# The compressed branch's output made turned and gated on the probabilities, and added by VectorE as it reads the attention's accumulator

## The reference, cut to what matters

```
s = einsum('bgrtd,bgcd->bgrtc', qh, kcmp) * scale
s = where(cmask, s - slopes * dcmp, NEG)
p_cmp = softmax(s, axis=-1) * cmask
o_cmp = einsum('bgrtc,bgcd->bgrtd', p_cmp, vcmp)
imp = einsum('bgrtc,cj->bgtj', p_cmp, overlap)      # picks the blocks of the selected branch
...
gt = sigmoid(gates.reshape(B, S, 3, G, R).transpose(2, 0, 3, 4, 1))[..., None]
o = gt[0] * o_cmp + gt[1] * o_sel + gt[2] * o_win
```

## Time and profile before

| | |
|---|---|
| Median of 3 runs | 3756.53 us (3756.47 to 3762.29) |
| The profiled execution | 3753.49 us |
| Its span, first to last instruction | 3751.6 us |
| Mean granted PE clock | 0.955 of full speed |
| PE busy | 3490.3 us (93%) |
| DVE busy | 1752.8 us (47%) |
| ACT busy | 871.6 us (23%) |
| POOL busy | 1041.0 us (28%) |

### The profile page before, as it was taken

The page is one execution under the profiler, slowest core; times in us unless marked ns, Lnnn a source line. Parts: engine busy times, 40 slices in busy tenths (PEclk is TensorE's granted clock), DMA queues, the critical chain, the costliest instruction groups (busy, mean ns, idle before and its releaser), DMA issues. The chain is left out here.

```text
span 3751.6 us, 55639 instructions
## 1 busy us (share of the span) xinstructions
PE 3490.3 (93%) x23230; PEld 2892.4 (77%) x23230; DVE 1752.8 (47%) x2597; ACT 871.6 (23%) x1261; POOL 1041.0 (28%) x498
## 2 busy tenths in 40 slices
PE   5999999989999889999999799978996899999997
PEld 4878888867888778888888677757784778888886
DVE  4762566424887535655555535234433322323223
ACT  2111222122444112111111220244431211111112
POOL 4332333343110442212122143221212422121221
PEclk7999999999999989999999899979997899999998
DMA  3453334342000422322222164310002111111111
GB/s 95 141 177 126 113 110 125 108 121 86 12 5 1 143 65 93 112 67 73 84 78 78 45 174 106 115 58 20 20 3 107 45 50 57 39 56 45 45 45 45
DMA packets 310492, 289.74 MB, mean 77 GB/s; under 512 B 21492, under 2 KB 277030, under 8 KB 309086
## 3 DMA queue, kind: packets, MB, share of 16 engines
q1 hardware_dynamic: 282992, 202.89, 18.4%
q10 hardware_dynamic: 26482, 82.06, 5.8%
q0 software_dynamic: 816, 1.88, 0.3%
HBM read 223.22 MB, written 63.57 MB: 76 GB/s over the span
## 5 line engine op out<-in xcount | busy, mean ns | idle before, releaser
L719 POOL TENSOR_TENSOR ffn_wlo<-ffn_raw,ffn_whi 128x1024 fp32r<-128x1024 f32 x88 | 211.2, 2402 | 1061.8 <-ACT ffn_whi L913 1006.1
L209 PE MATMUL up<-h_hi,ffn_whi 128*128 128x512 f32 x1408 | 438.4, 393 | 17.1 <-POOL h_lo L410 11.2
L209 PE MATMUL up<-h_lo,ffn_whi 128*128 128x512 f32 x1408 | 435.9, 391 | 0.0
L209 PE MATMUL up<-h_hi,ffn_wlo 128*128 128x512 f32 x1408 | 435.5, 391 | 0.0
L209 PE MATMUL acc<-h_hi,whi 128*128 128x512 f32 x1136 | 371.3, 408 | 46.7 <-POOL wlo L171 24.1
L209 PE MATMUL acc<-h_lo,whi 128*128 128x512 f32 x1136 | 355.3, 394 | 0.0
L209 PE MATMUL acc<-h_hi,wlo 128*128 128x512 f32 x1136 | 353.7, 393 | 0.0
L192 POOL TENSOR_TENSOR whi<-raw,ones 128x1024 fp32r<-128x1024 f32 (+1 forms) x83 | 156.9, 1890 | 698.5 <-PE acc L209 538.0
L209 PEld LDWEIGHTS up<-h_hi,ffn_whi 128*128 128x128 f32 x1408 | 264.1, 189 | 72.5 <-issue 11.7
L209 PEld LDWEIGHTS up<-h_hi,ffn_wlo 128*128 128x128 f32 x1408 | 265.7, 189 | 55.9
L209 PEld LDWEIGHTS up<-h_lo,ffn_whi 128*128 128x128 f32 x1408 | 265.5, 189 | 56.0
(11 more groups left out here) (551 smaller groups left out, 6105.6 us busy)
## 6 DMA issues: line engine op xcount, KB each, us to landing
raw<-w_in SPq DMA_DIRECT2D x51, 512.0 KB
projT<-proj_stage ACTq DMA_DIRECT2D x51, 512.0 KB, 3.1
ffn_ada_raw<-w_ada SPq DMA_DIRECT2D x24, 1024.0 KB, 5.0
ffn_raw<-w_up SPq DMA_DIRECT2D x44, 512.0 KB
ffn_draw<-w_down SPq DMA_DIRECT2D x11, 1024.0 KB, 6.7
ffn_raw<-ffn_w_gate SPq DMA_DIRECT2D x22, 512.0 KB
ffn_raw<-ffn_w_up SPq DMA_DIRECT2D x22, 512.0 KB
ffn_draw<-ffn_w_down SPq DMA_DIRECT2D x11, 1024.0 KB, 4.7
```

The costliest lines, as they stand in the source:

```text
L209: last = nc.tensor.matmul(acc[:, t, :], w[:, k, w_cols], x[:, k, t * HALF:(t + 1) * HALF], start=(k == 0 and i == 0), stop=(k == k_tiles - ...
L719: nc.gpsimd.tensor_tensor(w_lo[i][:], raw[i][:], w_hi[i][:], ALU.subtract).then_inc(s[f"up_split{i}"], 1)
```

## The change

The compressed output is made turned: in `tile_values` weights and moving operand change places, so the output has two heads' 64 features on the partitions and tokens along the row. A gate per token can then no longer be applied on reading it, so DVE multiplies the probabilities by the gate after the mask (`gated_p`, new, in the bias's buffer), and PE turns `gated_p` in place of `e`. The bias's load of the next tile waits until `gated_p` has been turned. `tile_output` becomes a copy. In the attention the product with the identity is gone; DVE adds `N["o"]` to the accumulator as it reads it, into a new buffer `att_sum` [128, 4, 1024]. For pairs 0 to 2 ACT makes `hi` of the whole pair (128x1024) and POOL `lo`, once both heads are done; pair 3 is split on DVE tile by tile, from `att_sum`.

```diff
@@ load_tile (SP)
                 sp.dma_start(qc, q).then_inc(s["q_in"], 16)
+                if i > 0:
+                    sp.wait_ge(s["probs_turned"], i)
                 sp.dma_start(bias[:], ins["k_cmpbias"][:, i]).then_inc(s["bias_in"], 16)
@@ turn_probs, tile_values (PE)
-                pe.wait_ge(s["p_done"], i + 1)
+                pe.wait_ge(s["p_gated"], i + 1)
                 for k in range(4):
-                    last = nc.tensor.transpose(side[:, k * P:(k + 1) * P], e[:, 2 * k:2 * k + 2, :].rearrange("p h c -> p (h c)"), ident[:])
+                    last = nc.tensor.transpose(side[:, k * P:(k + 1) * P], gated_p[:, 2 * k:2 * k + 2, :].rearrange("p h c -> p (h c)"), ident[:])
...
-                    last = nc.tensor.matmul(side[:, k * P:(k + 1) * P], pcT[:, k, :], vc[:, k // 2, :], start=True, stop=True)
+                    last = nc.tensor.matmul(side[:, k * P:(k + 1) * P], vc[:, k // 2, :], pcT[:, k, :], start=True, stop=True)
@@ tile_softmax, tile_output (DVE)
                 tt(e[:], e[:], cmask[:, i:i + 1, :].broadcast_to(wide), ALU.mult).then_inc(s["p_done"], 1)
+                dve.wait_ge(s["p_done"], i + 1)
+                gates = N_["gates"][:, i, 0:NSA_H].unsqueeze(2).broadcast_to(wide)
+                tt(gated_p[:], e[:], gates, ALU.mult).then_inc(s["p_gated"], 1)
...
-                gates = N_["gates"][:, i, 0:NSA_H].unsqueeze(2).broadcast_to([P, NSA_H, NSA_D])
-                tt(o_tile[:].rearrange("p (h d) -> p h d", d=NSA_D), side[:].rearrange("p (h d) -> p h d", d=NSA_D),
-                   gates, ALU.mult).then_inc(s["o_taken"], 1)
+                nc.vector.tensor_copy(o_tile[:], side[:]).then_inc(s["o_taken"], 1)
@@ nsa_attend, POOL
+            def low(p):
+                pool.wait_ge(s["pair_high"], p + 1)
+                nc.gpsimd.tensor_tensor(lo[:, p, :], att_sum[:, p, :], hi[:, p, :], ALU.subtract).then_inc(s["pair_split"], 1)
+
             for h in range(2, NSA_H):
                 split(h)
+                if h % 2:
+                    low(h // 2 - 1)
@@ nsa_attend, values (PE)
-                if r == 0:
-                    if h == 0:
-                        pe.wait_ge(s[f"o_in{i}"], 16)
+                if r == 0 and h * (NT // 2) + i // 2 > 0:
                     pe.wait_ge(s[f"o_read{i % 2}"], h * (NT // 2) + i // 2)
-                    nc.tensor.matmul(out, N["o"][:, i, h * NSA_D:(h + 1) * NSA_D], ident[:], start=True, stop=False)
...
-                                            start=False, stop=(r == 1 and t == tiles(i, r) - 1))
+                                            start=(r == 0 and t == 0), stop=(r == 1 and t == tiles(i, r) - 1))
@@ nsa_attend, ACT
+            def high(p):
+                for b in range(2):
+                    act.wait_ge(s[f"o_read{b}"], (2 * p + 2) * (NT // 2))
+                nc.scalar.activation(hi[:, p, :], att_sum[:, p, :], ACT.Copy).then_inc(s["pair_high"], 1)
+
...
                 if j + 2 < NJ:
                     exps(j + 2)
+                if j % (2 * PER_HEAD) == 5 and j > 5:
+                    high(j // (2 * PER_HEAD) - 1)
@@ nsa_attend, output (DVE)
                 out = ps[f"ob{i % 2}"][rows, 0:P]
-                steps.link(nc.vector.tensor_copy(hi[rows, p, c], out))
-                nc.vector.tensor_tensor(lo[rows, p, c], out, hi[rows, p, c], ALU.subtract).then_inc(s[f"o_read{i % 2}"], 1)
+                if h == 0:
+                    dve.wait_ge(s[f"o_in{i}"], 16)
+                nc.vector.tensor_tensor(att_sum[rows, p, c], out, N["o"][rows, i, p * P:(p + 1) * P], ALU.add).then_inc(s[f"o_read{i % 2}"], 1)
+                if p == 3:
+                    dve.wait_ge(s[f"o_read{i % 2}"], h * (NT // 2) + i // 2 + 1)
+                    steps.link(nc.vector.tensor_copy(hi[rows, p, c], att_sum[rows, p, c]))
+                    steps.do(nc.vector.tensor_tensor(lo[rows, p, c], att_sum[rows, p, c], hi[rows, p, c], ALU.subtract))
```

More of the change, by code:

```diff
@@ L1039, in projections_and_retention @@
     bias = mem.at("cmp_bias", 190, [P, NSA_H, NC_PAD])
+    gated_p = mem.at("cmp_gated", 190, [P, NSA_H, NC_PAD])
     o_tile = mem.at("cmp_o", 192, [P, NSA_H * NSA_D])
@@ L1060, in projections_and_retention @@
               "gate_row_in gates_on gates_turned gates_copied tables_in pg_cleared q_in bias_in scores_done scores_taken exp_in exp_done "
-              "p_done probs_turned probs_copied o_done o_taken o_stored sel_ready sel_turned sel_copied sel_stored "
+              "p_done p_gated probs_turned probs_copied o_done o_taken o_stored sel_ready sel_turned sel_copied sel_stored "
               "vrow_in vrow_turned vrow_copied ") + RMS_SEMS
@@ L2107, in nsa_attend @@
     probT = [mem.at(f"att_probT{r}", 124 + 8 * r, [P, NT, P]) for r in range(2)]
+    att_sum = mem.at("att_sum", 88, [P, 4, S])
     small = [mem.at(f"att_small{r}", 204 + 0.5 * r, [P, 4]) for r in range(2)]
     raw, w_hi, w_lo = (x[0][:, 0:4, :] for x in mem.weights)
-    names = both("q_in q_split scores_done max_done exp_done inverted scaled grouped group_copied o_done o_read") + "o_in0 o_in1 o_in2 o_in3 o_in4 o_in5 o_in6 o_in7 vector_step pool_step weight_loaded weight_high weight_split"
+    names = both("q_in q_split scores_done max_done exp_done inverted scaled grouped group_copied o_done o_read") + "o_in0 o_in1 o_in2 o_in3 o_in4 o_in5 o_in6 o_in7 vector_step pool_step weight_loaded weight_high weight_split pair_high pair_split"
     banks = [(f"sc{r}", [P, S], F32) for r in range(2)] + [(f"{n}{r}", [P, HALF], F32) for n in ("pt", "ob") for r in range(2)]
```

## The result

The changed kernel takes 3774.56 us (median of 7 runs, 3765.33 to 3777.94) against 3757.22 us for the kernel before beside it (7 runs, 3752.93 to 3770.6): a ratio of 1.0033, interval 1.0020 to 1.0046. It is slower by some 12 us: the medians differ by 17.3, the means (3772.6 and 3760.1) by 12.5. The forecast was 3757.9 with a range to 3768, so the time lies outside the range, on the side to which I had given 0.12. The profiled execution took 3775.72 us (span 3773.9); its granted clock is 0.956 of full speed, as before.

A forecast was written before the change was run, and what follows sets the result against it. It took TensorE, waiting on VectorE's softmax, to bound the projections, and the VectorE-ScalarE loop the attention. Terms summed to +1.4 us on the profiled 3753.49, 3754.9; plus 3.0 for the median, 3757.9, range 3745 to 3768 (8 in 10).

The forecast's parts named there:

- The gate's product, +5.8: Projections: the added VectorE product between mask and transposes is uncovered in all eight tiles, 0.72 us each, +5.8 us.
- Attention's first head, -3.3: Attention's first head: without the identity products VectorE waits less for TensorE, less 1.5 for meeting GpSimd, -3.3 us.
- Six passages, -3.0: Six head-to-head passages with GpSimd's query split: at most 1.2 us gained, port contention leaves 0.5 each, -3.0 us.
- The slower rival: GpSimd's first piece blocks the 1024-column scaling at all six passages, +0.9 each; 3771.8 us in all, chance 0.12.
- The wide subtractions, +1.7: Attention, heads 2, 4 and 6: GpSimd's three output subtractions hold the port against about one scaling each, +1.7 us.
- The +0.4 for ScalarE's casts: Attention, heads 2, 4 and 6: three high parts made on ScalarE, mostly in its free time, +0.4 us.
- Last pair on VectorE, +1.0: Attention, last pair: output split takes three VectorE operations instead of two, bare at each head's start, +1.0 us.
- Seventh passage, -1.3: Passage into the last head, without GpSimd work: a lead of six TensorE products gained, -1.3 us.
- After the last reciprocal: Attention's end: last TensorE product saved, -0.2 us; the last job's extra VectorE operation bare, +0.3 us.
- TensorE sets the pace: Attention: TensorE bounds it, so the removed products pay in full, -14.0; 3746.2 us, chance 0.2 of over 7.5 faster.
- The port takes it back: Attention: GpSimd blocks scalings at six passages, +8.4, and three subtractions cost +5.5; sum +15.3, 3771.8 us, chance 0.12.
- The gate's product is hidden: Projections: the added VectorE product costs nothing; -4.4 us in all, 3752.1 us, chance 0.05.

The follow-up runs named there:

- Without the split: Changed kernel with GpSimd's query split for heads 2 to 7 left out (stale queries reused): attention stage 352.5 us.
- in pieces: Changed kernel with GpSimd's query split and its wide subtractions each issued in four column pieces: 3761.59 us, ratio 1.0009 to the kernel before.
- best: Changed kernel with GpSimd's query split and wide subtractions in four column pieces, mask product for the first query tile alone: 3760.1 us, ratio 1.0007.
- best2: As best, but gated probabilities made by one product from the unscaled ones, scaled ones afterwards: 3755.46 us, ratio 0.9983.
- changed, padded: Changed kernel with 127 more waits on TensorE at the program's start: 3770.63 us, ratio 1.0032.
- attention's part alone: Kernel before with only the attention's hunks of the diff, compressed output reaching it unturned: ratio 1.0012.
- projections' part alone: Kernel before with only the projections' hunks of the diff, attention as before: ratio 1.0013.
- before, single mask product: Kernel before with the compressed branch's mask product made for the first query tile alone: 3756.38 us, ratio 0.9992.
- before, padded: Kernel before with 127 more waits on TensorE at the program's start: 3760.07 us, ratio 1.0010.

## Why the prediction was wrong

**The gate's product, +5.8: right.** +5.8 us in the profiled execution, 11.9 - 6.0 = 5.9 us of waits. The product takes 0.69 us and the idle before the transposes grew by 0.72 in each of the eight tiles, in six of them from 0.49 to 1.21. Over four profiles of each the stage grew by 6.6, for two of the changed kernel's lie 2 us above the others. The bias load, the turned product and the copy cost nothing that shows: the load came 0.7 us behind the transposes and nobody waited for it.

**Attention's first head, -3.3: right in kind.** Two of its turns went from 4.37 to 2.41 and from 3.94 to 2.21 us, the head without its last two turns from 36.6 to 32.4, -4.2 in the first profile. Over four profiles of each it went from 35.6 to 32.6 us, -3.0.

**Six passages, -3.0: this is the first step that failed.** I take the five turns around each passage, from reciprocal to reciprocal. Before, the six take 12.71 to 12.85 us, 76.6 in all; in the changed kernel four take 13.49 to 13.51 and two 12.00 and 11.89, 77.9 in all: +1.3. In the four the 1024-column scaling was blocked, and each lost 0.8 us; the two where it escaped gained 0.8 each. The slower rival had +0.9 for a blocked passage, so the price was known. Two things in the step were wrong. I gave a blocked passage only half the weight, from a margin of 0.46 us read at one passage, where three of the six had about 0.24. And I let the later scalings give back some 0.7 us after such a loss, so that of the 1.2 gained 0.3 were left; they did not give it back: the 640-column one was blocked for 2.18 us as before, on top of the new block. TensorE's lead was also smaller than the 0.65 us worked out: GpSimd's start moved by 0.41 to 0.44 us against the scaling at the four blocked passages. Over four profiles of each, with four or five passages blocked, the six went from 76.6 to 78.6 us, +2.0 instead of -3.0. Without the split they take 69.4, so the block is what turned a gain of 1.2 us a passage into a loss.

**The wide subtractions, +1.7.** The turns they meet took 0.45, 0.45 and 1.24 us more than in the kernel before, 2.1 in all. The +0.4 for ScalarE's casts was not measured by itself. **Last pair on VectorE, +1.0**: head 7 from its fourth turn on went from 30.5 to 31.1 us, +0.6. **Seventh passage, -1.3**: its five turns went from 12.71 to 12.15, -0.6. **After the last reciprocal**, where the sum had +0.1, the stage went from 40.0 to 38.5 us, -1.5.

So the attention came out at -2.4 us in the first profile, where the sum had -4.4, and over four profiles of each at 361.6 before and 361.8 after, no gain at all. The two sites give +6.8 instead of +1.4. With that alone the forecast would have been 3763.3, within the range; what took the time out of it lies behind the attention and in the base.

**What no step had, and the second that failed: the second block.** The sum put everything behind the attention at nothing without giving a reason. The timed difference is 11 to 12 us, the two sites hold 6.8. The rest is behind them. For each kernel I set the difference of its mean time from the kernel before's against the difference of its first stage and attention stage together (from the kernel before's four profiles; the changed kernel's is the mean of four too, each other kernel has one):

| kernel | timed | two stages | left over |
|---|---|---|---|
| changed (12 runs) | +11.2 | +6.8 | +4.4 |
| in pieces (10) | +3.3 | -1.7 | +5.0 |
| `best` (10) | +0.6 | -5.5 | +6.1 |
| `best2` (12) | -6.1 | -10.3 | +4.2 |
| changed, padded (7), less 4.1 for its waits at the start | +10.0 | +9.9 | +0.1 |
| attention's part alone (12) | +3.1 | +3.4 | -0.3 |
| projections' part alone (12) | +5.5 | +7.3 | -1.8 |
| before, single mask product (12) | -3.6 | -2.8 | -0.8 |
| before once more (12) | +2.5 | 0.0 | +2.5 |
| before, padded (10), less 4.2 for its waits | -2.6 | -1.1 | -1.5 |

Four of the five kernels with both parts lose 4 to 6 us somewhere else, and the fifth nothing; of the five without both parts four come out at -1.8 to -0.3, and the kernel before set against itself at +2.5. Each figure has some 2 to 3 us of error: the runs of one kernel have a standard deviation of 3 to 7 us, and all but the first row take the two stages from one profile. The means are +4.0 and -0.4, so a loss of some 4 us behind the two sites is likely, and no single row shows it. The recurrence stage agrees: 521.3 us in the mean of ten profiles with both parts, 515.2 in ten without. Dealt to the two groups at random, these twenty lengths would differ by as much about once in 60 times; the stages between and behind differ by under 2 us in the mean. That the stage's length follows its granted clock is measured. Why it meets the lower grant more often when both parts are in is open, and that both parts cause it is not shown: neither a part alone, nor the moment (the projections' part alone reaches the stage at 2470.71 us, later than the changed kernel's 2466.36, and takes 512.5), explains it, and the profiles of 513.7 (padded) and 507.3 (`best`) show that it is a matter of how often. I did not try to hold the clock.

**The rivals.** "TensorE sets the pace" fell with the run that took 64 products away and got longer. "The port takes it back" was the truest of the cases, given 0.12: the attention's half of it came about in a milder form, and the sites gave +6.8 where it had +15.3. That the time of 3774.56 came within 2.8 of its 3771.8 is luck: the tail, which no case had, and a base that was too low filled the gap. "The gate's product is hidden" fell at once. My range ended at 3768 because every term ended at the attention's end. Of the 16.7 us between forecast and median, 5.4 are the two sites, some 4 the tail, 3.5 the base (3756.53, where the seven runs of the kernel before have a mean of 3760.1), and 2.0 the median's distance from its own mean; the rest is within the error of these figures.

Most of what I had named as a sign of being right came about: the idle before the transposes, the 5.8 us, and VectorE's waits for ScalarE (99 turns). VectorE's waits for the accumulator did not vanish: 9.4 us in 11 turns, where there were 13.8 in 19. None of the signs looked past the attention. Repeats of the kernel before reach from 3744.57 to 3777.18 us over 95 runs; the three runs shown beforehand, within 6 us, hid that.

## What to carry to other kernels

Before pricing work taken from an engine that is nearly always busy, ask who starts when it has finished, and what that one collides with: here the products saved moved GpSimd's start over a VectorE instruction, and 64 of them were worth nothing until GpSimd's instructions were cut. A margin by which two instructions miss each other is to be read at every place where they meet, and not at one. Where two engines exclude each other for the length of an instruction, cut the instruction of the one that has time to spare into pieces; four pieces gave back 8 us for 16 us more of GpSimd's own time. A product placed on the path at which the bounding engine already waits costs its full length each time: first look for one on that path that need not be there.

## What the runs showed of the hardware that was not expected

Three things. The length of one stage of 8504 small products moved between 507.3 and 525.6 us, with its mean granted clock between 0.90 and 0.86, in a program whose mean clock over the whole run showed nothing of it (0.953 in the profile with 507.3, 0.956 in the first with 525); over twenty profiles, two edits more than a thousand microseconds earlier went with a shift of 6 us in the mean, and whether they cause it is open. A VectorE scaling that starts up to 0.08 us ahead of a GpSimd instruction in the profile is still the one that is blocked (2.48 to 2.52 us for 0.81); from 0.21 us on it runs free. And a GpSimd instruction that is cut in four takes three tenths longer in all (5.41 us for 4.19), and still the kernel gains, since the scalings beside it fell from 2.49 to 1.22 us.
